# One layer of a two-block transformer kernel on one Trainium2 core: norm factors moved into the weights, one split of the token tiles for all projections, entry tile by tile, fewer barriers

## The reference

```python
def rms_norm_2(x, g):                       # per token: x / sqrt(mean(x*x) + EPS) * g
    return x * lax.rsqrt(jnp.mean(x * x, -1, keepdims=True) + EPS) * g

kv = rms_norm_2(x, kv_norm) @ w_kv_shared   # (512, 1536): keys K, values V, 12 heads of 64
k_s, v_s = jnp.split(kv, 2, axis=-1)
proj = rms_norm_2(x, b_norm[0]) @ b_w_in[0]
q, qm, gate = jnp.split(proj, [768, 1024], axis=-1)
o = stick_breaking_attention(q, k_s, v_s)
# in memory_attention:
kvm = rms_norm_2(mem, mem_norm[1]) @ mem_w_kv[1]      # (256, 512): keys and values of the memory
om = softmax(rms(qm) @ rms(keys)^T / 8) @ values      # 4 heads
x = x + concat([o, om]) * silu(gate) @ b_w_out[0]
```

## Time and profile before

| | us |
|---|---|
| median of 3 runs | 3559.25 (3558.64 to 3562.4) |
| the profiled execution: its own time | 3566.67 |
| its span, first to last instruction | 3564.5 |
| PE busy in the span | 3192.7 (90%) |
| DVE, ACT, POOL busy | 1946.9, 1005.4, 914.4 |
| mean granted clock of TensorE | 0.935 of full speed |

### The profile page before, as it was taken

The page is one execution under the profiler, slowest core; times in us unless marked ns, Lnnn a source line. Parts: engine busy times, 40 slices in busy tenths (PEclk is TensorE's granted clock), DMA queues, the critical chain, the costliest instruction groups (busy, mean ns, idle before and its releaser), DMA issues. The chain is left out here.

```text
span 3564.5 us, 37534 instructions
## 1 busy us (share of the span) xinstructions
PE 3192.7 (90%) x15004; PEld 2484.3 (70%) x15004; DVE 1946.9 (55%) x2904; ACT 1005.4 (28%) x1774; POOL 914.4 (26%) x596
## 2 busy tenths in 40 slices
PE   7998989999999999979898999799979788787698
PEld 4976656777488888877665664588879556676476
DVE  3576764444755555655674655567576656233354
ACT  3135760000221111222563001322221145411352
POOL 1004764221200000010576441100010435004263
PEclk9999999999999999989999999899989779798799
DMA  6411004343121122041112553322213200112100
GB/s 198 159 38 27 19 19 144 106 116 106 59 71 71 48 71 71 24 155 37 26 36 85 141 144 124 110 95 95 95 48 97 96 1 13 42 65 83 51 1 24
DMA packets 208413, 268.23 MB, mean 75 GB/s; under 512 B 29312, under 2 KB 136784, under 8 KB 207728
## 3 DMA queue, kind: packets, MB, share of 16 engines
q1 hardware_dynamic: 206160, 265.83, 23.3%
q10 hardware_dynamic: 2080, 0.01, 0.0%
HBM read 255.17 MB, written 10.52 MB: 75 GB/s over the span
## 5 line engine op out<-in xcount | busy, mean ns | idle before, releaser
L734 POOL TENSOR_TENSOR ht_lo<-HT,ht_hi 128x1024 fp32r<-128x1024 f32 x28 | 68.5, 2445 | 1107.0 <-ACT ht_hi L716 733.1
L1853 PE MATMUL ps<-ht_hi,w_hi 128*128 128x512 f32 (+1 forms) x768 | 273.8, 357 | 14.1 <-issue 12.5
L1853 PE MATMUL ps<-ht_lo,w_hi 128*128 128x512 f32 (+1 forms) x768 | 273.2, 356 | 0.0
L1853 PE MATMUL ps<-ht_hi,w_lo 128*128 128x512 f32 (+1 forms) x768 | 272.9, 355 | 0.0
L1863 PE MATMUL ps<-w_hi,a_hi 128*128 128x512 f32 x640 | 251.1, 392 | 4.3 <-DVE a_lo L1970 4.3
L1863 PE MATMUL ps<-w_lo,a_hi 128*128 128x512 f32 x640 | 250.0, 391 | 0.0
L1863 PE MATMUL ps<-w_hi,a_lo 128*128 128x512 f32 x640 | 249.9, 390 | 0.0
L364 PE MATMUL ps<-w_lo,ht_hi 128*128 128x320 f32 (+2 forms) x800 | 245.7, 307 | 0.0
L364 PE MATMUL ps<-gate_ht_hi,gate_w_hi 128*128 128x512 f32 (+1 forms) x576 | 227.3, 395 | 16.7 <-POOL w_lo L387 16.7
L1477 POOL TENSOR_TENSOR p_lo<-ring,p_hi 128x512 fp32r<-128x512 f32 x156 | 199.8, 1291 | 116.1 <-DVE p_hi L1432 88.1
L364 PE MATMUL ps<-U,ring 128*128 128x512 f32 (+1 forms) x576 | 217.9, 521 | 0.0
(11 more groups left out here) (401 smaller groups left out, 7965.6 us busy)
## 6 DMA issues: line engine op xcount, KB each, us to landing
ring<-w_dram SPq DMA_DIRECT2D x30, 2048.0 KB, 8.1
U<-w_ada_dram SPq DMA_DIRECT2D x80, 512.0 KB, 3.7
ring<-w_in_dram SPq DMA_DIRECT2D x48, 512.0 KB, 6.5
ring<-w_in_dram SPq DMA_DIRECT2D x8, 1280.0 KB, 5.9
ring<-a_w_in_dram SPq DMA_DIRECT2D x8, 1280.0 KB, 6.7
ring<-w_ada_dram SPq DMA_DIRECT2D x4, 2048.0 KB, 10.7
hi_scratch<-ht_hi SPq DMA_DIRECT2D x2, 3072.0 KB, 10.8
gate_ht_hi<-hi_scratch SPq DMA_DIRECT2D x8, 768.0 KB, 4.4
```

The source lines that it names most:

```text
L734: pool.tensor_tensor(HT_LO[:, :, tokens], HT[:, :, tokens], HT_HI[:, :, tokens].bitcast(F32), ALU.subtract).then_inc(ht_ready.sem, 1)
L1853: last = pe.matmul(ps[:, g % 4, 0:c1 - c0], lhsT, rhs, start=(k + j == 0), stop=(k == KD - 1 and j == 2))
```

## The change

- The square roots of `x` and `mem` come tile by tile. As DVE adds the second half of tile t of layer 0's output it goes on with its variance and scaling (`Entry.norm`), and PE turns tiles 0 and 1 inside the output product's last loop, tiles 2 and 3 inside the first groups of V, tiles 4 and 5 (`mem`) before V's seventh and eighth group.
- A turned tile of `x` is copied out without any factors, as hi and as full value (`Entry.place`, 6 instructions on ACT), and POOL takes the remainder (`Entry.rest`). This one split serves V, K, qm, Q and the gates. `rms_to_ht` and both `split_operand` are gone.
- The factors are multiplied into the weights: by DVE ahead of the rounding of each piece, for V's first slot by POOL (`scaled`) with the rounding on ACT (`weights_rounded`) and the remainder on POOL (`weights_rest`).
- The order is now V, K, then `mem` (4 groups) and qm (4 groups) in one gemm of 256 columns with split operands, Q, gates. The gates' weights are split by DVE, no longer by POOL. The norms of the memory heads stand on DVE behind the split of Q's first slot.
- The barriers of layer 1's projections and around `softmaxes` go. Waits on `evac_done`, `heads_normed`, `turn_taken` and `ht_ready` take their place. The constants are loaded ahead (`constants_load`), and the sticks' table is rounded inside `softmaxes(1)`. `sticks` starts its first two score groups before it waits for the last output of the softmaxes.
- Buffers move accordingly (K, the memory's keys and values, the sticks' buffers and some output weights); that part is left out below.

```diff
-                            if name == "vector":
+                            if scale[s] is not None:
+                                by = gains[:, scale[s], q * KD // pieces:(q + 1) * KD // pieces]
+                                w3 = w.rearrange("p (k n) -> p k n", k=KD // pieces)
+                                dve_chain.link(eng, eng.tensor_tensor(w3, w3, bc(by, 2, cols[s] // KD), ALU.mult))
...
-def rms_to_ht(tiles, outs):
...
                     for k in self.order:
                         self.products(pe, 1, t, k)
+                    if entry and t >= 2:
+                        entry.turn(pe, t - 2)
...
+                        if entry and i:
+                            dve_chain.link(dve, last)
+                            entry.norm(dve, t)
...
+    def norm(self, dve, t):
+        if t == XT:
+            dve.wait_ge(mem_back.sem, 16)
+        spread(dve, self.p, t, EPS, t, True)
+        if 2 <= t < XT:
+            dve.wait_ge(turn_done.sem, self.p.turned + t - 1)
+        dve.tensor_scalar(self.source(t), X[:, t, :], RSTD[:, t:t + 1], None, ALU.mult).then_inc(xn_ready.sem, 1)
+    def place(self, act, t):
+        act.wait_ge(turn_done.sem, self.p.turned + t + 1)
+        tokens = slice(t * P, (t + 1) * P)
+        four = [ps[:, self.bank(t) + i, :].rearrange("p (k n) -> p k n", n=P) for i in range(2)]
+        if t < XT:
+            first = B_FIRST[:, :, tokens], B_NEXT[:, :, tokens]
+            act.activation(first[0], four[0], ACT.Copy)
+            act.activation(first[1], four[1][:, 0:2, :], ACT.Copy)
+            for k in (6, 7):
+                act.activation(B_HI[k][:, tokens], four[1][:, k - 4, :], ACT.Copy)
+            for i in range(2):
+                last = act.activation(HT[:, 4 * i:4 * i + 4, tokens], four[i], ACT.Copy)
+        else:
+            for k in range(KD):
+                act.activation(HT[:, k, tokens], four[k // 4][:, k % 4, :], ACT.Identity, scale=gains[:, 4, k:k + 1])
+                last = act.activation(MEM_HI[:, k, (t - XT) * P:(t - XT + 1) * P], four[k // 4][:, k % 4, :],
+                                      ACT.Identity, scale=gains[:, 4, k:k + 1])
+        last.then_inc(turn_taken.sem, 1)
+    def rest(self, pool, t):
+        pool.wait_ge(turn_taken.sem, self.p.taken + t + 1)
+        tokens = slice(t * P, (t + 1) * P)
+        x, lo = HT[:, :, tokens], HT_LO[:, :, tokens]
+        if t < XT:
+            pool.tensor_tensor(lo[:, 0:4], x[:, 0:4], B_FIRST[:, :, tokens].bitcast(F32), ALU.subtract)
+            pool.tensor_tensor(lo[:, 4:6], x[:, 4:6], B_NEXT[:, :, tokens].bitcast(F32), ALU.subtract)
+            for k in (6, 7):
+                last = pool.tensor_tensor(lo[:, k], x[:, k], B_HI[k][:, tokens].bitcast(F32), ALU.subtract)
...
+    def scaled(self, pool, q):
+        if q == 0:
+            pool.wait_ge(ring_full[0].sem, self.loaded[0])
+        w = slot(0, KD, 384)[:, 2 * q:2 * q + 2, :]
+        pool.tensor_tensor(w, w, bc(gains[:, 2, 2 * q:2 * q + 2], 2, 384), ALU.mult).then_inc(w_scaled.sem, 1)
+    def weights_rounded(self, act, q):
+        act.wait_ge(w_scaled.sem, q + 1)
+        c = slice(q * 768, (q + 1) * 768)
+        act.activation(B_W[0][:, c], ring[0][:, c], ACT.Copy).then_inc(w_rounded[0].sem, 1)
+    def weights_rest(self, pool, q):
+        pool.wait_ge(w_rounded[0].sem, self.rounded + q + 1)
+        c = slice(q * 768, (q + 1) * 768)
+        pool.tensor_tensor(LO[0][:, c], ring[0][:, c], B_W[0][:, c].bitcast(F32),
+                           ALU.subtract).then_inc(w_split[0].sem, 1)
...
-    with block(not pairs) as b:
+    with block(False) as b:
...
-            if pairs:
-                sp.dma_start(RR, A["causal"]).then_inc(loaded.sem, 16)
-            else:
-                sp.dma_start(STICKS_IN, A["sticks"]).then_inc(loaded.sem, 16)
...
-            pe.wait_ge(ones_ready.sem, ones_ready.n + 1)
-            for kind, c, i in early("piece", "maximum", "row"):
+            pe.wait_ge(evac_done.sem, evac_done.n)
+            pe.wait_ge(heads_normed.sem, heads_normed.n)
+            for n, (kind, c, i) in enumerate(early("piece", "maximum", "row")):
+                if n == 2:
+                    pe.wait_ge(ones_ready.sem, ones_ready.n + 1)
...
+                if not pairs and g == 2:
+                    dve.wait_ge(constants_loaded.sem, constants_loaded.n)
+                    dve.tensor_scalar(ZEROS[:, :], cst[:, 1:2].to_broadcast([P, P]), 0.0, None, ALU.mult)
+                    dve.tensor_copy(STICKS[:, :], CONSTANTS_IN[1]).then_inc(sticks_ready.sem, 1)
...
-            pe.wait_ge(ones_ready.sem, ones_ready.n + 1)
+            pe.wait_ge(sticks_ready.sem, 1)
             scores(0)
             scores(1)
+            pe.wait_ge(o_taken.sem, o_0)
...
-    nc.scalar.wait_ge(mem_back.sem, 16)
-    nc.vector.wait_ge(mem_back.sem, 16)
-    rms_to_ht(range(NT), lambda t: [(ht_part(t), 3), (HK[:, :, t * P:(t + 1) * P], 2)] if t < XT
-              else [(ht_part(t), 4)])
-    project2(range(XT, NT), 256, HT, MK[1])
-    split_operand(HK, B_HI, HK_LO, S)
-    split_hk = B_HI, HK_LO
-    features(3, split_hk, K6, ACT.Copy, KV_W, hi=K6H, lo=K6L)
-    project2(range(XT), 384, split_hk, V2, KV_W)
-    project2(range(XT), 128, HT, QM2)
-    split_operand(HT, B_HI, HT_LO, S)
-    split_ht2 = B_HI, HT_LO
-    features(3, split_ht2, Q6, ACT.Copy, B_W, hi=Q6H, lo=Q6L, scale=HD ** -0.5)
-    normed_heads(4, split_ht2, GT[1], B_W,
-                 [(heads(QM2), gains64[:, 4, :]), (heads(MK[1][:, :, 0:MEM_W]), gains64[:, 5, :])])
+    constants_load(0)
+    normed_heads(4, split_ht2, GT[0], A_W, [(heads(P2[:, :, 3 * DIFF_W:]), gains64[:, 2, :]),
+                                            (heads(MK[0][:, :, 0:MEM_W]), gains64[:, 3, :])])
+    entry = softmaxes(0, P2[:, :, 3 * DIFF_W:], Out(0))
+    values_and_entry(entry)
+    split_b = B_HI, B_LO
+    def mem_placed(pe, g):
+        if g in (0, 2):
+            pe.wait_ge(turn_taken.sem, entry.p.taken + XT + 1 + g // 2)
+    def banks_free(pe, g):
+        if g == 0:
+            pe.wait_ge(evac_done.sem, evac_done.n)
+    features(3, split_b, K6, ACT.Copy, B_W, hi=K6H, lo=K6L, gain=2, join=False, ready=mem_placed)
+    memory_and_queries(split_b, entry)
+    norms = HeadNorms([(heads(QM2), gains64[:, 4, :]), (heads(MK[1][:, :, 0:MEM_W]), gains64[:, 5, :])], [])
+    made = evac_done.n
+    def behind(dve, slot_index):
+        if slot_index == 0:
+            dve.wait_ge(evac_done.sem, made)
+            norms.squares(dve, range(2))
+            norms.means(dve)
+            norms.normed(dve)
+            norms.gained(dve)
+            dve.sem_inc(heads_normed.sem, 1)
+    def beside(act, g):
+        if g == 2:
+            norms.root(act)
+    heads_normed.n += 1
+    features(3, split_b, Q6, ACT.Copy, B_W, beside=beside, hi=Q6H, lo=Q6L, scale=HD ** -0.5, gain=3, join=False,
+             behind=behind)
+    constants_load(1)
+    features(4, split_b, GT[1], ACT.Silu, B_W, join=False, gain=3, ready=banks_free)
     out = Out(1)
     softmaxes(1, QM2, out)
     sticks(out)
+def values_and_entry(entry):
+    def ready(pe, g):
+        if g in (0, 1):
+            entry.turn(pe, g + 2)
+        pe.wait_ge(ht_ready.sem, entry.p.ht + g + 1)
+    def between(pe, n):
+        if n in (6, 7):
+            entry.turn(pe, n - 2)
+    def behind(dve, slot_index):
+        if slot_index == 1:
+            for t in range(XT, NT):
+                entry.norm(dve, t)
+    def beside(act, slot_index, g):
+        if slot_index == 1 and g >= 2:
+            root(act, entry.p, g + 2, g + 2)
+        if slot_index == 1 and g == 3:
+            entry.place(act, XT)
+    with block(False) as b:
+        @b.scalar
+        def _(act):
+            for t in range(XT):
+                root(act, entry.p, t, t)
+                if t:
+                    entry.weights_rounded(act, t - 1)
+                    entry.place(act, t - 1)
+            entry.weights_rounded(act, XT - 1)
+            entry.place(act, XT - 1)
+        @b.gpsimd
+        def _(pool):
+            entry.scaled(pool, 0)
+            for q in range(1, 4):
+                entry.scaled(pool, q)
+                entry.weights_rest(pool, q - 1)
+            entry.weights_rest(pool, 3)
+            for t in range(XT):
+                entry.rest(pool, t)
+    project2(range(XT), 384, (B_HI, B_LO), V2, B_W, False, ready, 4, behind, beside, 2, (None, "vector"), between)
+    with block(False) as b:
+        @b.scalar
+        def _(act):
+            entry.place(act, XT + 1)
+        @b.gpsimd
+        def _(pool):
+            for t in range(XT, NT):
+                entry.rest(pool, t)
+def memory_and_queries(split_b, entry):
+    def mms(s, g, d):
+        if s == 0:
+            t, c = XT + g % 2, g // 2 * 256
+            m = slice((g % 2) * P, (g % 2 + 1) * P)
+            return [(d, 256, [p for k in range(KD) for p in parts(
+                MEM_HI[:, k, m], MEM_LO[:, k, m], *weight_parts(0, B_W, 512, k, c, c + 256))])]
```

(19 more changed lines are left out.)

192 lines of the change are left out of this document (96 added, 96 removed).

## The result

| | before, us | after, us |
|---|---|---|
| median, both kernels on the same chip (4 runs each) | 3558.94 (3557.79 to 3562.4) | 3502.51 (3496.41 to 3511.83) |
| ratio, with its 95% interval | | 0.9842 (0.9825 to 0.986) |
| profiled execution: own time, span | 3566.67, 3564.5 | 3496.41, 3494.6 |
| mean granted clock | 0.935 | 0.95 |

What follows compares the result with a forecast made beforehand. PE, busy 90% of the span, was taken as the bound, so time is gained where it stands still or runs at the low clock. Projections 50.5 plus starts 15.3 gave 65.8 us, median 3493, range 3482 to 3511.

Steps and rivals of the forecast that it cites:

- K: Layer 1's K projection: six groups of 5.44 us, 32.6 us, no restart since DVE's first pieces fall into V's last group.
- memory and qm: Eight 256-column groups with split operands: 23.0 us plus 1.2 for the wait on K's last evacuation.
- Q: Q projection, 42.3 us: 32.6 of products, 1.7 late at first pieces, 8 late in the second slot behind the memory norms.
- gates: Layer 1's gates: 1.2 us wait plus 43.5 of products, with DVE's pieces done during Q's second slot.
- starts: Barriers and late constants gone at softmaxes(0), softmaxes(1) and sticks: 7.5, 1.7 and 6.1 us sooner, together 15.3.
- The entry: Before V's first product: ACT's program order, then POOL's last remainders, make V start 12.1 us after the third turn.
- V's two turns: Turns 4 and 5, in V: each waits 2.9 us for a root behind ACT's evacuation; 5.8, plus 2 for the clock.
- rival (a): Entry: six POOL instructions each wait out one of DVE's, 5.8 us; K's first pieces wait, 1.5 reaching PE; 3499; chance 0.20.
- Rival (b): The three starts: other waits stand in for the barriers, 13 of the 15.3 us are lost; 3506 us; chance 0.09.
- (c): Memory heads' root early: Q loses 3 us instead of 9.7, turns 4 and 5 cost no clock; 3484; chance 0.07.
- (d): V's first weights: POOL's repeated-factor products slow; gain used up at 21 us each, 3571 at 24; chance 0.02.
- The total: Whole kernel: 65.8 us saved, profiled execution from 3566.7 to 3500.9, median to 3493 us; chance 0.61.

Runs made afterwards that it cites:

- again: The changed kernel run once more, unedited: 3505.24 us, ratio 0.9831 to the kernel before.
- entry_order: The changed kernel with only the order of POOL's and ACT's work at the entry changed: 3493.88 us, ratio 0.9802 to the kernel before.
- roots_early: The changed kernel with ACT taking the memory tiles' two roots two evacuations of V earlier: 3487.23 us, ratio 0.9783 to the kernel before.
- rest_late: The changed kernel with POOL taking the memory tiles' remainders only after DVE's first four K weight pieces: 3502.25 us, ratio 0.9823 to the kernel before.
- norms_late: The changed kernel with the memory heads' norms behind Q's second weight slot, their root one evacuation later: 3503.65 us, ratio 0.9823 to the kernel before.
- norms_gates: The changed kernel with the memory heads' norms behind the gates' first weight slot: 3499.25 us, ratio 0.9816 to the kernel before.
- starts_back: The changed kernel with the barriers at the three starts, and the constants' load behind them, put back: 3516.96 us, ratio 0.9861 to the kernel before.
- best: The changed kernel with entry_order, roots_early, rest_late and norms_gates together: 3477.85 us, ratio 0.9758 to the kernel before.

## Why the prediction was right or wrong

| step | forecast, us | measured in after |
|---|---|---|
| V's first product, after the end of layer 0's output (3067.5 in before, 3052.9 in after, see the result) | 14.8 | 15.7 (at 3068.60) |
| V's last evacuation, from there too | 61.2 | 60.8 |
| K | 32.6 | 37.8 (again: 34.2) |
| memory and qm | 24.2 | 24.5 |
| Q; of it late in the second slot | 42.3; 8 | 43.2; 8.8 |
| gates | 44.7 | 45.4 |
| sum, saved of the projections | 205.0; 50.5 | 211.6; 44.1 |
| starts | 7.5 + 1.7 + 6.1 | 8.1 + 1.8 + 6.9 |

**The entry** was right in place, releaser and length, a wait of 12.67 us where I had 12.1, but two of its terms erred against each other. ACT had rounded the last quarter 8.2 us after that point instead of 8.9, and POOL needed 2.55 + 4.9 behind it instead of 1.84 + 2.8 + 1.2. One term more was too small without harm: DVE's scalings of tiles 1 to 3 took 2.3 us and not 0.75, each beside an instruction of POOL's (tile 0's, with POOL idle, took 0.75), so that DVE needed 6.05 us a tile. ACT waited only 0.2 us for root 3 by it. What I didn't ask is whether the order itself is needed: entry_order shows that V ends 9.4 us sooner by order alone, 7.8 of it at the entry.

**V's two turns** waited 2.3 us each, forecast 2.9, released by DVE's X as the text says; roots_early shows the mechanism and its clock, 6.6 us together against my 7.8.

**K** is the step that failed. "No restart, since DVE's first pieces fall into V's last group" put K at its pure product time, 32.6 us; it took 37.8. DVE's pieces did begin there, but POOL's two remainders of the memory tiles met two of the casts, 2.05 us more each, and PE waited 0.30, 0.80 and 2.83. That was rival (a)'s last clause, priced there at 1.5; it measured 3.9 in after and 0.8 in again, and rest_late takes it away. A group of 512 columns takes 5.49 us in the changed kernel and not 5.44, which is 0.3 more. I had costed DVE's pieces by their own lengths and let POOL's work next to them cost nothing in the main sum.

**Rival (a)** otherwise fell: POOL's six instructions at the entry grew by 2.8 us together beside DVE's split, which is more than my 1.2 and half of the rival's 5.8, and V began 0.9 late, not 4.6.

**Q** was right in mechanism and size: the gap lies in the second slot, PE waits 5.32 us for DVE's piece and then 0.80, and norms_late and norms_gates move it. The text said that the norms had been covered beside the gates before. In the changed kernel the gates cover them again, all but 1.7 us, if they stand behind the gates' first slot and not ahead of it. For Q's first slot the prediction charged 1.7 us; its own numbers give 1.1 (the fourth piece is ready at 9.35 + 3 x 2.45 = 16.7 us, PE wants it at 11.5 + 3 x 1.36 = 15.6), and PE's wait there was 0.8.

**The starts** were right within 1 us each. Rival (b) is refuted by starts_back, in which 16.2 us come back.

**Rivals (c) and (d)** didn't come: the memory heads' root stood where I put it, and POOL's products with the repeated factor took 1.45 to 1.92 us each, not 21.

**The total.** In the profiled executions I forecast 3500.9, and it was 3496.4. That is closer than it deserves: the changed places gave 60.9 instead of 65.8, and 9.0 came from code that didn't change. In again, whose own start lay 4.2 us later than after's, the span is 66.5 below the span of before. The median came out 9.5 higher than forecast: 4.9 are what the changed places fell short, and 4.5 more are the difference between their 60.9 and the 56.4 of the medians. On the chip of again the medians are 60.9 apart. That agrees with the profile's sum to 0.1 us, which is partly luck: the interval of that ratio is 13 us wide. The step from a profile to a median is good to 5 us at best. The 7.4 by which before's profile lay above its median was such a step too; after's profile lay 6.1 below its own.

## What to carry to other kernels

Ahead of a stage that waits, write out each engine's program order and ask of every instruction whether what stands before it feeds the same consumer: three reorderings, without one instruction less, gave best's 24.7 us (the wait that rest_late adds shows nothing more in K beside them). A step that moves needs other work of PE's to hide behind at its new place, and what counts is when PE wants the first piece behind it: the same norms cost 8.8, 5.3 or 1.7 us in three places. Where POOL has a long instruction, keep DVE's casts from beginning inside it (0.56 against 2.6 us here); an earlier start of DVE does this as well as a later one of POOL.
